# Mixture of experts on one core: the overflow block between the two projections, its own release of weight chunks, and biases beside the transposes

## What is computed

```python
logits = xt @ w_router + b_router                     # 256 tokens, 32 experts
top_logits, top_idx = lax.top_k(logits, 4)
top_w = jax.nn.softmax(top_logits, axis=-1)
# for each expert e, over the tokens that chose it:
gate, up = jnp.split(xb @ w_gu[e] + b_gu[e], 2, axis=-1)
gate = jnp.minimum(gate, 7.0)
up = jnp.clip(up, -7.0, 7.0)
act = (up + 1) * (gate * jax.nn.sigmoid(1.702 * gate))
y[token] += top_w[token, e] * (act @ w_dn[e] + b_dn[e])
```

## Time and profile before

| what | value |
|---|---|
| time, median of 3 runs (lowest, highest) | 2419.94 us (2419.78, 2422.48) |
| the profiled execution: its time | 2423.33 us |
| its span, first to last instruction | 2420.8 us |
| mean granted TensorE clock | 0.961 |
| PE busy | 2175.9 us, 90% of the span |
| DVE, ACT, POOL busy | 768.4, 471.8, 65.7 us |
| the chain that ended last | PE 80%, DMA 6%, DVE 5%, ACT 4%, issue 2% |
| transfers, mean over the span | 244 GB/s; 418 GB/s in the slices where they never pause |

### The profile page before, as it was taken

One profiled execution on the slowest core, in us unless ns is written; L12 is line 12 of the kernel. 1 busy time (PEld: TensorE's weight loads), 2 busy tenths in 40 slices (PEclk: granted clock), 3 DMA queues, 4 the chain that ended last, 5 costly groups with the idle time before them and its releaser, 6 DMA issues.

```text
span 2420.8 us, 29069 instructions
## 1 busy us (share of the span) xinstructions
PE 2175.9 (90%) x11393; PEld 1153.6 (48%) x11394; DVE 768.4 (32%) x1859; ACT 471.8 (19%) x915; POOL 65.7 (3%) x79
## 2 busy tenths in 40 slices
PE   5999986899999998999889985997979996999997
PEld 4844453333333333333333334744454445888873
DVE  1596242122222221222212213242023254787101
ACT  1011101111111111111111101032011115887100
POOL 0000000000000000000000001000000000212000
PEclk8999987999999999999999997999989997999999
DMA  9544564769999998999957995443233141221240
GB/s 341 203 156 174 215 234 199 326 265 418 418 418 418 418 418 333 418 418 418 418 218 304 418 391 199 149 150 128 105 117 139 70 148 70 73 103 70 99 173 24
DMA packets 158838, 591.28 MB, mean 244 GB/s; under 512 B 5307, under 2 KB 6911, under 8 KB 125871
## 3 DMA queue, kind: packets, MB, share of 16 engines
q1 hardware_dynamic: 152496, 573.08, 60.4%
q0 software_dynamic: 4384, 16.40, 1.9%
q10 hardware_dynamic: 1887, 0.81, 0.1%
HBM read 589.23 MB, written 1.05 MB: 244 GB/s over the span
## 4 chain that ended last, share of the span: by engine, by line
PE 80%; DMA 6%; DVE 5%; ACT 4%; issue 2%; DVEq 2%; ACTq 0%; SPq 0%
PE PS L587 24%; PE PS L847 17%; PE PS L575 10%; PE PS L869 9%; PE PS L1032 4%; DMA W<-in_w_gu 3%; PE PS L881 2%; DMA W<-in_w_dn 2%; PE PS L840 1%; PE PS L1102 1%; PE PS L804 1%; PE PS L632 1%; DVE BIG L1808 1%; PE PS L817 1%; DVE BIG L1804 1%
## 5 line engine op out<-in xcount | busy, mean ns | idle before, releaser
L587 PE MATMUL PS<-W,BIG 128*128 128x512 f32 x1344 | 584.8, 596 | 5.0 <-DVE BIG L2213 2.9
L847 PE MATMUL PS<-W,BIG 128*64 128x512 f32 x2048 | 451.6, 598 | 3.5 <-DMA W<-in_w_gu 3.5
L587 PEld LDWEIGHTS PS<-W,BIG 128*128 128x128 f32 x1344 | 256.4, 191 | 323.8 <-issue 317.2
L847 PEld LDWEIGHTS PS<-W,BIG 128*64 128x64 f32 x2048 | 145.0, 138 | 309.5 <-issue 300.9
L575 PE MATMUL PS<-BIG,W 128*128 128x256 f32 x1088 | 238.1, 381 | 2.1 <-ACT BIG L345 2.1
L869 PE MATMUL PS<-W,BIG 128*64 128x512 f32 x1024 | 229.4, 601 | 8.4 <-ACT BIG L1294 8.4
L575 PEld LDWEIGHTS PS<-BIG,W 128*128 128x128 f32 x1088 | 207.5, 191 | 32.3 <-ACT BIG L345 3.2
L1802 DVE TENSOR_SCALAR BIG<-PS 128x512 f32<-128x512 f32 (+1 forms) x38 | 24.7, 650 | 424.7 <-PE PS L847 378.6
L869 PEld LDWEIGHTS PS<-W,BIG 128*64 128x64 f32 x1024 | 71.1, 138 | 146.2 <-issue 128.8
L1290 ACT ACTIVATE BIG<-BIG 128x512 f32<-128x512 f32 x32 | 20.2, 630 | 492.9 <-DVE BIG L1802 492.9
L632 PE MATMUL PS<-K,BIG 128*128 128x128 f32 (+2 forms) x193 | 36.6, 355 | 77.6 <-DVEq L1858 23.3
(11 more groups left out here) (453 smaller groups left out, 1916.3 us busy)
## 6 DMA issues: line engine op xcount, KB each, us to landing
W<-in_w_gu SPq DMA_DIRECT2D x128, 2048.0 KB, 14.2
W<-in_w_dn SPq DMA_DIRECT2D x64, 2048.0 KB, 15.8
W<-in_w_in SPq DMA_DIRECT2D x24, 2048.0 KB, 8.1
W<-in_w_mod SPq DMA_DIRECT2D x12, 2048.0 KB, 9.8
W<-in_gla_w_in SPq DMA_DIRECT2D x10, 2048.0 KB, 7.9
W<-in_s_w_in SPq DMA_DIRECT2D x8, 2048.0 KB, 8.9
W<-in_s_w_glu SPq DMA_DIRECT2D x8, 2048.0 KB, 8.2
W<-in_w_out SPq DMA_DIRECT2D x6, 2048.0 KB, 8.1
```

The costliest lines, as they stand in the source:

```text
L587: ins = pe.matmul(ps[:, t, :], lhs(i * KT + k)[:, t * P:(t + 1) * P], w[:, k, :], start=i + k == 0, stop=last_chunk and k == KT - 1)
L847: ins = pe.matmul(PS[hh[h], g, :], XET[:, k, :], gu_w(k)[:, g * D + h * CH:g * D + (h + 1) * CH], start=False, stop=k == KT - 1, skip_grou ...
```

## The change

On PE the overflow blocks move from the head of an expert to the place between gate-up and the gather of the next expert's rows; they wait for the ordinary activation first. Since the ordinary gate-up has then waited for chunks 0 to 3, the block doesn't wait for these again. The block counts `x_chunk_done` at each chunk that it is through with, and SP waits for both counts: six numbers per expert, computed from the table on DVE (TABX), are read into SP's registers. The ordinary count is as before. The biases of the next expert (`gate_bias`) move from its head to behind the transposes of the expert before, and wait for the two SELB copies by `selb_ready`. On ACT and DVE the blocks move to the same place, behind the sigmoid and behind `swiglu`. The block's activation gets a buffer of its own (ACTVX). Ahead of the loop the zeros and biases of three of the four banks no longer wait for the table, which DVE now computes behind the first one-hot; the fourth bank, where the counts lie, still does. Two pairs of semaphores become one each, with the same waits.

```diff
+        TABX = MISC[0:1, 2 * P:2 * P + 6 * NE].rearrange("p (j e) -> p j e", j=6).bitcast(I32)
...
+                        freed = [] if previous is None else [x_freed(previous, j) for j in range(6)]
                         for j in range(6):
                             sp.wait_ge(chunk_done, e * 6 + (pre + j - RING + 1))
+                            if previous is not None:
+                                sp.wait_ge(ev("x_chunk_done"), freed[j])
...
+                    load_expert(0, None)
+                    sp.wait_ge(ev("table_ready"), 1)
+                    with sp.Fori(1, NE) as e:
+                        load_expert(e, e - 1)
...
             def extra_block(x, e):
+                pe.wait_ge(ev("act_ready"), e + 1)
...
-                    if k % 2 == 0:
-                        landed(e, k // 2)
...
+                    if k % 2 == 1 and k < KT - 1:
+                        ins.then_inc(ev("x_chunk_done"), 1)
...
-            def expert(e, last):
-                extras(e)
+            def gate_bias(e):
+                pe.wait_ge(ev("selb_ready"), e + 1)
                 for h in range(2):
                     for g in range(2):
                         pe.matmul(PS[hh[h], g, :], SELB[half_rows[g], :], BGU[half_rows[g], h * CH:(h + 1) * CH],
...
                 ins.then_inc(ev("up_done"), 1)
+                extras(e)
                 if not last:
                     gather_rows(e + 1, False)
...
                 if not last:
                     turn_rows(e + 1)
+                    gate_bias(e + 1)
...
+            for q in range(3):
+                zero_sum(q)
             gather_rows(0, True)
+            pe.wait_ge(ev("wmt_ready"), 1)
+            for q in range(3):
+                bias_sum(q)
             turn_rows(0)
+            pe.wait_ge(ev("table_ready"), 1)
+            zero_sum(3)
+            bias_sum(3)
+            gate_bias(0)
             turn_scatter(0)
...
             def expert(e, last):
-                extras(e)
                 act.wait_ge(ev("gate_clipped"), e + 1)
                 act.activation(SG, GT, ACT.Sigmoid, scale=1.702).then_inc(ev("sig_gate"), 1)
+                extras(e)
...
             def expert(e, last):
-                extras(e)
                 if not last:
                     one_hot(e + 1, K[:, C_SLOT:C_SLOT + BLK], PW, G, GW, ev("g_ready"))
-                swiglu(ev("gate_done"), ev("gate_clipped"), ev("sig_gate"), ev("up_done"), e + 1, ev("act_ready"), CH)
+                swiglu(ev("gate_done"), ev("gate_clipped"), ev("sig_gate"), ev("up_done"), e + 1, ev("act_ready"), CH,
+                       ACTV)
+                extras(e)
...
+            for j in range(6):
+                dve.tensor_scalar(TABX[:, j, :], TABF[:, 1, :], 6.0, float(j + 1), ALU.mult, ALU.add)
+            dve.drain()
+            dve.sem_inc(ev("x_chunk_done"), 6)
+            dve.sem_inc(ev("table_ready"), 1)
```

More of the change, by code:

```diff
@@ L358, in _, with x_freed, load_expert @@
                 if kind == "moe":
-                    with sp.Fori(0, NE) as e:
+                    def x_freed(e, j):
+                        return sp.value_load(TABX[0:1, j, bass.ds(e, 1)] if not isinstance(e, int) else TABX[0:1, j, e:e + 1],
+                                             min_val=1, max_val=6 * 64 + 6)
+                    def load_expert(e, previous):
                         gu = A["w_gu"][0, bass.ds(e, 1)].rearrange("e (k p) n -> p (e k) n", p=P)
                         dn = A["w_dn"][0, bass.ds(e, 1)].rearrange("e (k p) n -> p (e k) n", p=P)
+                        freed = [] if previous is None else [x_freed(previous, j) for j in range(6)]
                         for j in range(6):
                             sp.wait_ge(chunk_done, e * 6 + (pre + j - RING + 1))
+                            if previous is not None:
+                                sp.wait_ge(ev("x_chunk_done"), freed[j])
                             flat_w = W[:, j].rearrange("p k n -> p (k n)")
@@ L371, in _ @@
                                     .then_inc(w_landed[j], 16)
+                    load_expert(0, None)
+                    sp.wait_ge(ev("table_ready"), 1)
+                    with sp.Fori(1, NE) as e:
+                        load_expert(e, e - 1)
+                    after_moe = [x_freed(NE - 1, j) for j in range(6)]
                     continue
@@ L661, in _ @@
             mod_spread("sh1")
-            pe.wait_ge(ev("h1_ready"), 1)
+            pe.wait_ge(ev("h_ready"), 1)
             h1 = row(HN)
@@ L718, in _ @@
             mod_spread("g2")
-            pe.wait_ge(ev("h2_ready"), 1)
+            pe.wait_ge(ev("h_ready"), 2)
             rows_to_columns("h2", [H2[:, 0], H2[:, 1]])
@@ L739, in _, with zero_sum, bias_sum @@
             ins.then_inc(ev("pos_done"), 1)
-            pe.wait_ge(ev("wmt_ready"), 1)
-            pe.wait_ge(ev("table_ready"), 1)
-            for q in range(4):
+            def zero_sum(q):
                 pe.matmul(PS[:, 4 + q, :], ZW, H2[:, 0, 0:CH], start=True, stop=False, skip_group_check=True)
-            for q in range(4):
+            def bias_sum(q):
                 for t in range(TT):
@@ L818, in extra_block @@
                                         start=k == 0, stop=k == KT - 1, skip_group_check=True)
+                    if k == 3:
+                        ins.then_inc(ev("x_chunk_done"), 1)
                 ins.then_inc(ev("x_down_done"), 1)
@@ L825, in extra_block @@
                                         start=False, stop=False, skip_group_check=True)
+                        if t == 0 and q == 0:
+                            ins.then_inc(ev("x_chunk_done"), 1)
                 ins.then_inc(ev("x_scattered"), 1)
@@ L841, in expert @@
                                   start=True, stop=False, skip_group_check=True)
+            def expert(e, last):
                 for k in range(KT):
@@ L1299, in _ @@
             copy_rows(0)
+            act.wait_ge(ev("table_ready"), 1)
             with act.Fori(0, NE - 1) as e:
@@ L1755, in _ @@
             dve.scalar_tensor_tensor(POS, pos[:, 0:2, :], 1.0, SEL, ALU.add, ALU.mult)
-            cnt, nx = pos[0:1, 2, :], TABF[:, 0, :]
-            dve.tensor_scalar(nx, cnt, float(BLK), None, ALU.is_gt)
             dve.drain()
             dve.tensor_scalar_add(POS, POS, -1.0)
-            for j in range(1, XMAX):
-                dve.scalar_tensor_tensor(nx, cnt, float(BLK + j * XBLK), nx, ALU.is_gt, ALU.add)
-                dve.drain()
-            dve.tensor_tensor_scan(TABF[:, 1, :], ONES[0:1, 0:NE], nx, 0.0, ALU.mult, ALU.add)
             dve.drain()
-            dve.tensor_tensor(TABI[:, 0, :], TABF[:, 1, :], nx, ALU.subtract)
-            dve.tensor_copy(TABI[:, 1, :], TABF[:, 1, :])
-            dve.drain()
-            dve.sem_inc(ev("table_ready"), 1)
             def one_hot(e, io, pw, g, gw, done):
@@ L1797, in scatter_of, with swiglu @@
                 dve.tensor_copy(SC, PS[:, 3, 0:T]).then_inc(ev("sc_ready"), 1)
-            def swiglu(gate, clipped, sig, up, n, ready, width):
+            def swiglu(gate, clipped, sig, up, n, ready, width, dst):
                 w = slice(0, width)
@@ L1807, in swiglu @@
                 dve.drain()
-                dve.scalar_tensor_tensor(ACTV[:, w], UP[:, w], 1.0, GT[:, w], ALU.add, ALU.mult).then_inc(ready, 1)
+                dve.scalar_tensor_tensor(dst, UP[:, w], 1.0, GT[:, w], ALU.add, ALU.mult).then_inc(ready, 1)
             def extra_block(x, e, j):
@@ L1839, in _ @@
             one_hot(0, K[:, C_SLOT:C_SLOT + BLK], PW, G, GW, ev("g_ready"))
+            cnt, nx = pos[0:1, 2, :], TABF[:, 0, :]
+            dve.tensor_scalar(nx, cnt, float(BLK), None, ALU.is_gt)
+            dve.drain()
+            for j in range(1, XMAX):
+                dve.scalar_tensor_tensor(nx, cnt, float(BLK + j * XBLK), nx, ALU.is_gt, ALU.add)
+                dve.drain()
+            dve.tensor_tensor_scan(TABF[:, 1, :], ONES[0:1, 0:NE], nx, 0.0, ALU.mult, ALU.add)
+            dve.drain()
+            dve.tensor_tensor(TABI[:, 0, :], TABF[:, 1, :], nx, ALU.subtract)
+            dve.tensor_copy(TABI[:, 1, :], TABF[:, 1, :])
+            for j in range(6):
+                dve.tensor_scalar(TABX[:, j, :], TABF[:, 1, :], 6.0, float(j + 1), ALU.mult, ALU.add)
+            dve.drain()
+            dve.sem_inc(ev("x_chunk_done"), 6)
+            dve.sem_inc(ev("table_ready"), 1)
             columns_of(0)
```

22 lines of the change are left out of this document (13 added, 9 removed).

## The result

The changed kernel takes 2409.73 us in the median of seven runs (2406.58 to 2417.93), the kernel before 2422.48 beside it (seven runs, 2419.78 to 2427.86): a ratio of 0.995, 95% interval 0.9935 to 0.9964. That is 12.7 us, and faster, but under half of the 31.0 forecast, and 2409.73 lies just outside the range that ended at 2408. The profiled execution took 2406.64 us with a span of 2404.8, against 2423.33 and 2420.8; PE is busy for 2177.0 us in it (2175.9 before), and of the chain that ended last PE has 78%, DMA 9%, issue 2%.

A forecast was written before the change was run, and what follows sets the result against it. The expert stage was taken as bound by TensorE's own instructions, with weights just behind. Gains of 10.7, 1.2, 0, 14.8 and 10.6 less 6.3 made 31.0 us: 2389 from the 2419.94 median, range 2380 to 2408.

The forecast's parts named there:

- Entry: Ahead of the first expert: sums no longer wait for the table, gate-up at about 392.7 instead of 403.45; gain 10.7 us.
- First expert: Gate-up falls from 15.76 to 13.95 us, 0.6 lost to loads and branch now behind it; net gain 1.2 us.
- Ordinary experts: Head's 1.36 us removed, 1.33 added ahead of down; period stays at 28.66 us, bounds 0.6 shorter to 0.4 longer.
- Blocks: Overflow block between gate-up and gather: 2.33 us pause, then 17.72; 1.27 us more in five experts, loss 6.3.
- the rival of 2399 to 2409: Pauses cost blocks their clock (1.7 us each, 10 in all), longer period, cold entry; gain only 11 to 21; chance 0.17.
- a longer period: Part of the pauses and half clock rival: period 0.4 us longer in some 15 experts TensorE bounds, 6 us.
- a cold entry: Part of the pauses and half clock rival: a cold entry ahead of the first expert costs 4 us.
- Weights: Blocks free chunks early, load queue restarts sooner: some 11 of 15.9 us of waits go, plus 3.9 half clock; gain 14.8.
- the hand-over: Blocks' early freeing of weight chunks, 14.8 us; rival that it brings nothing: 2404 us, chance 0.05.
- Last expert: From the previous scatter to its own end 30 us instead of 40.6, 3.7 idle ahead of its transposes; gain 10.6 us.
- The sum: All terms: 10.7 + 1.2 + 0 - 6.3 + 14.8 + 10.6 = 31.0 us gained.
- Branch stalls in the loop: Rival: the moved branch stalls in each of 31 experts, 19 to 99 us lost, 2408 to 2488 us; chance 0.07.

The follow-up runs named there:

- run with early loads: Changed kernel with TensorE's two register loads moved after three of the gate-up's eight steps, only the branch left behind gate-up: 2404.32 us, 0.9928 of the kernel before.
- the pause filled: Changed kernel with idle matmuls ahead of the block's wait for the activation, in two runs: 4.56 us of them, 2411.98 us; cut to 2.43 us, 2397.83 us.

## Why the prediction was right and wrong

**Entry: right.** 10.7 forecast; 13.4 in the two traces, of which 2.4 arose ahead of the stage (the sums' predecessors start that much earlier), so 11.0. From the first sum to gate-up it is 13.46 us, and 13.5 was forecast.

**First expert: the branch mis-sized.** I put it at 3.4 us, the 5.31 of idle time at the old entry less the loads' 1.9, and so only 0.6 lost. It lasts 6.28 there (3.98 idle), and the gather behind it ran at half clock. The first expert takes 33.3 us where 29.3 was forecast. At its old place the 3.4 was nearly right: the trace before has 3.70 for that branch. What failed is that I carried it over to the new place, where the first branch takes 5.9 to 6.6 in all runs; why it is longer there no run shows. The 6.07 in the same row was the better figure. The run with early loads shows loads and branch in a row, less the lead.

**Ordinary experts: right.** 28.66 forecast, 28.44 measured, within the bounds. But that the biases' new place earns its keep, none of the runs shows: with them back at the head the period is 28.27.

**Blocks: the step that failed.** The 2.33 us of pause came as forecast (2.35, five times). That the work behind it keeps its clock, which the 17.72 carried over from the old place took as given, did not: gate-up took 8.06 to 9.49 in four of the five blocks that follow a pause, and down 5.35 in the fifth. With the pause filled, all gate-ups took 7.11, in both runs. The earlier trace rows had shown the loss in one place, and I had it as a rival at 1.7 a block, with a chance of 0.17. The filled pause prices it at 10.2 us in the five experts, 2.0 each, and 10 to 12 in the medians. So the rival of 2399 to 2409 named the cause, and 2409.73 lies just past its far end. But its other parts, a longer period and a cold entry, did not come; the first expert and the weights cost about as much instead, so that its time fits so nearly is luck.

**Weights: right in kind, its size half seen.** Chunk 0 behind expert 2's blocks went out at 492.10 (forecast 489.3), behind 16's at 924.25 (914.8). The first is 2.8 late, by the first expert's 4 us and the block's half clock less the earlier entry. The second is 9.5 late: these 2.8; 3.4 more from the first issue until 16's last gate-up chunk lands (418.3 us where 414.9 was forecast), while chunks 3 and 4 were held and the DMA share fell to 0.71 and 0.81 between 508 and 512 us; and 3.2 in 16's own block, at half clock. That chunks 0 to 3 need only the two gate-ups was wrong: chunk 3 waits for the transposes behind the block. Lifting that hold alone won nothing, and no run lifts chunk 4's. Waits fell from 15.9 to 9.4 instead of 5, none in blocks. What the hand-over is worth I had as 14.8; taken back, it costs 27, since the block's new place without it is worse than the old one (28.2 us of waits against 15.9).

**Last expert: right.** 30 forecast, 31.6 measured, with 3.46 idle against 3.7, and the half clock (9.97 for down) that I had allowed for.

**The sum.** Between the first expert's end and the last one's start I forecast 8.5 us of gain (14.8 less 6.3); the traces show a loss of 3.6 (990.97 us from expert 1's gate-up to the end of expert 30's scatter before, 994.60 to the last gate-up after). These 12.1 us, the first expert's 3.9 and the last one's 1.6, less the 0.3 that the entry brought beyond its forecast, are the gap of 17.3 between 31.0 and the 13.7 that this pair of executions shows in the stage (16.1 less the 2.4 ahead of it).

Most of the 12.1 is the clock. Groups of PE in the stage, the block's gate-up and down projection before, then its down projection after:

```profile
L804 PE MATMUL PS<-W,BIG 128*32 128x256 f32 x768 | 44.6, 388 | 8.9 <-DMA W<-in_w_gu 5.3 <-DVE BIG L1812 3.6
L817 PE MATMUL PS<-W,BIG 128*32 128x256 f32 x384 | 26.7, 434 | 9.5 <-DMA W<-in_w_dn 7.1 <-ACT BIG L1274 2.4
```

```profile
L835 PE MATMUL PS<-W,BIG 128*32 128x256 f32 x384 | 25.3, 423 | 2.8 <-ACT BIG L1308 2.8
```

With the gather, biases and transposes ahead of gate-up (15.3 before, 18.5 after) the blocks' operations took 86.6 us before and 93.6 after: 7.0 more, where 3.9 less was forecast. The waits for weights fell by 6.5 instead of 11. Together that is some 15 us short, of which the ordinary experts' shorter period gave back 5. What stays open is the 2 us that are left, and how much of the waits is the blocks' doing, since a block that is later frees its chunks later.

**Branch stalls in the loop: did not come.** The median of 32 stays at 208 ns, with the long ones at the ends alone.

## What to carry to other kernels

When a step is moved to where its engine first has to wait, price the clock behind the wait with the wait itself: here 2.35 us of idle time cost about as much again (2.0 an expert), and moving the step's own first operations into the pause gave back 14 us. When a step is the last reader of a buffer, let it free the buffer piece by piece: that one edit was worth 27 us and turned a slower kernel into a faster one. And where a second bound stands close behind the first, as the weight queue does here, a saving of 0.4 us per expert can vanish into its waits.

## What the hardware showed that I had not expected

- Ten matmul passes of 128x512 with 128 columns of weights took 4.56 us; they start one by one, 0.43 us apart. Gate-up passes, 128x512 with 64 columns, took 13.95 us for 64: they go to two halves of the result's rows and start in pairs, 7 ns apart, a pair every 0.43 us. So the two of a pair overlap.
- TensorE falls to 1.2 GHz behind short pauses: 2.35 us for the activation, then a start of the block with little work, and 0.50 is granted from 1250.5 to 1254.5. With the pause filled, the gate-up at that place took 7.12 us in place of 9.26.
- In the changed kernel the first pass over the branch takes 6.28 us, the one in the last expert's own code 6.44, a repeated one 0.21; in the kernel before, the first took 3.70 and the last 6.07. With the loads earlier the first one took 6.39, so its earlier start was worth nearly its full lead: 1.65 of the loads' 1.9 us.
